# Hybrid streaming-encoder block on one core: the two halves of the normed input, element by element beside each other

## What is computed

```python
h = x + 0.5 * rmsnorm(swiglu(rmsnorm(x, g1), w_gate, w_up, w_down), g1_post)     # D_FF = 5632
z = rmsnorm(h, g_mix) @ w_in                                                     # 2048 x 5120
y = concat(gelu(gate) * rg_lru(conv4(lru_x)), sc_b * conv3(sc_c * sc_x)) @ w_out
h = h + rmsnorm(y, g_mix_post)
h = h + 0.5 * rmsnorm(swiglu(rmsnorm(h, g2), w_gate2, w_up2, w_down2), g2_post)
```

## Time and profile before

| | |
|---|---|
| median of 2 runs | 1818.22 us (1818.16 to 1818.27) |
| the profiled execution, its span | 1816.7 us |
| PE busy | 1799.5 us, 99% of the span, 8066 matmuls |
| PEld busy | 1486.2 us, 82%, 8066 weight loads |
| DVE busy | 940.9 us, 52% |
| ACT busy | 847.9 us, 47% |
| POOL busy | 20.2 us, 1% |
| HBM | 341.91 MB read, 189 GB/s over the span; DMA engines 61% |

### The profile page before, as it was taken

One profiled execution on the slowest core, in us unless ns is written; L12 is line 12 of the kernel. 1 busy time (PEld: TensorE's weight loads), 2 busy tenths in 40 slices (PEclk: granted clock), 3 DMA queues, 4 the chain that ended last, 5 costly groups with the idle time before them and its releaser, 6 DMA issues.

```text
span 1816.7 us, 22683 instructions
## 1 busy us (share of the span) xinstructions
PE 1799.5 (99%) x8066; PEld 1486.2 (82%) x8066; DVE 940.9 (52%) x990; ACT 847.9 (47%) x1023; POOL 20.2 (1%) x21
## 2 busy tenths in 40 slices
PE   8999999999999999999999999999999999999998
PEld 6888888888888888788888878888888888888886
DVE  5545444454454445655686465545445445445444
ACT  6544444444434334566654456444444444434442
POOL 0000000000000000100000010000000000000000
PEclk9999999999999999999999999999999999999999
DMA  7666666666565566675565656666666666556554
GB/s 229 215 191 193 190 188 193 186 188 192 176 199 189 171 203 204 188 211 173 164 196 174 199 160 231 186 189 192 185 186 191 189 187 192 176 177 216 189 184 148
DMA packets 179189, 344.69 MB, mean 190 GB/s; under 512 B 10685, under 2 KB 12869, under 8 KB 178757
## 3 DMA queue, kind: packets, MB, share of 16 engines
q1 hardware_dynamic: 179108, 344.04, 60.7%
q10 hardware_dynamic: 32, 0.01, 0.0%
HBM read 341.91 MB, written 2.10 MB: 189 GB/s over the span
## 4 chain that ended last, share of the span: by engine, by line
PE 98%; ACT 0%; DVE 0%; DMA 0%; issue 0%; POOL 0%; DVEq 0%; SPq 0%; ACTq 0%
PE ps L858 32%; PE ps L860 32%; PE ps L859 32%; PE ps L945 1%; PE ps L894 1%; PE ps L986 0%; PE ps L998 0%; DMA resid<-in_x 0%; DVE xT_lo L617 0%; ACT xT_hi L405 0%; POOL rstd L340 0%; ACT w_hi L383 0%; ACT act_g L387 0%; DVE resid L607 0%; DVEq L96 0%
## 5 line engine op out<-in xcount | busy, mean ns | idle before, releaser
L583 DVE TENSOR_TENSOR w_lo<-raw,w_hi 128x1024 fp32r<-128x1024 f32 x636 | 776.5, 1224 | 824.2 <-ACT w_hi L383 821.2
L383 ACT CAST w_hi<-raw 128x1024 fp32r<-128x1024 f32 x640 | 670.3, 1053 | 853.6 <-PE ps L860 829.5
L858 PE MATMUL ps<-w_hi,xT_hi 128*128 128x512 f32 x1728 | 679.0, 393 | 2.5 <-DVE xT_lo L617 2.5
L860 PE MATMUL ps<-w_hi,xT_lo 128*128 128x512 f32 x1728 | 674.0, 390 | 0.0
L859 PE MATMUL ps<-w_lo,xT_hi 128*128 128x512 f32 x1728 | 673.4, 390 | 0.0
L858 PEld LDWEIGHTS ps<-w_hi,xT_hi 128*128 128x128 f32 x1728 | 325.0, 188 | 69.1 <-issue 3.3
L860 PEld LDWEIGHTS ps<-w_hi,xT_lo 128*128 128x128 f32 x1728 | 324.9, 188 | 68.5
L859 PEld LDWEIGHTS ps<-w_lo,xT_hi 128*128 128x128 f32 x1728 | 325.1, 188 | 66.2
L858 PE MATMUL ps<-w_hi,hT_hi 128*128 128x512 f32 x832 | 327.5, 394 | 0.0
L860 PE MATMUL ps<-w_hi,hT_lo 128*128 128x512 f32 x832 | 326.3, 392 | 0.0
L859 PE MATMUL ps<-w_lo,hT_hi 128*128 128x512 f32 x832 | 323.6, 389 | 0.0
(11 more groups left out here) (77 smaller groups left out, 314.7 us busy)
## 6 DMA issues: line engine op xcount, KB each, us to landing
raw<-in_ffn_w_gate SPq DMA_DIRECT2D x176, 512.0 KB, 4.4
raw<-in_ffn_w_up SPq DMA_DIRECT2D x176, 512.0 KB, 3.5
raw<-in_ffn_w_down SPq DMA_DIRECT2D x176, 512.0 KB, 4.8
raw<-in_w_in SPq DMA_DIRECT2D x80, 512.0 KB, 3.8
raw<-in_w_out SPq DMA_DIRECT2D x32, 512.0 KB, 4.8
resid<-in_x SPq DMA_DIRECT2D x8, 256.0 KB, 8.8
gpost<-in_ffn_post_g SPq DMA_DIRECT2D x2, 1024.0 KB, 6.5
out<-resid SPq DMA_DIRECT2D x8, 256.0 KB, 2.8
```

The costliest lines, as they stand in the source:

```text
L383: sc.copy(w_hi[:, s], raw[:, s]).then_inc(hi_ready, 1)
L583: ve.tensor_tensor(w_lo[:, s], raw[:, s], w_hi[:, s].bitcast(f32), ALU.subtract).then_inc(lo_ready, 1)
L858: te.matmul(dst, xh, w_hi[:, s, k], start=start and k == 0, stop=False)
L860: last = te.matmul(dst, xl, w_hi[:, s, k], start=False, stop=stop and k == GK - 1)
```

## The change

The two tensors become two views of one. Element 0 of the last, innermost dimension is the high half and element 1 the low half of the same number:

```diff
@@ -104,8 +104,8 @@
         raw = sb("raw", [P, SLOTS, GK, W])
         w_hi = sb("w_hi", [P, SLOTS, GK, W], f32r)
         w_lo = sb("w_lo", [P, SLOTS, GK, W], f32r)
-        xT_hi = sb("xT_hi", [P, KD, T], f32r)
-        xT_lo = sb("xT_lo", [P, KD, T], f32r)
+        xT = sb("xT", [P, KD, T, 2], f32r)
+        xT_hi, xT_lo = xT[:, :, :, 0], xT[:, :, :, 1]
         resid = sb("resid", [P, TOK, D])
         gpost = sb("gpost", [P, D])
         act_g = sb("act_g", [P, TOK, W])
```

## The result

The changed kernel takes 1850.24 us (median of 2 runs, 1849.93 to 1850.56) where the kernel before took 1818.22. The ratio is 1.0179, with a 95% interval of 1.0161 to 1.0196: 32.0 us more, slower beyond doubt, though by a little under 2%. The profiled execution has a span of 1848.1 us, 31.4 us more than before's.

The account below looks back on a forecast made before the run. The prediction took the kernel as bound by PE's stream of matmuls. It summed 1816.7 + 0 for the loads + 1 for the writes = 1817.7 us profiled, so 1819 for timed runs, range 1815 to 1892.

Parts of the forecast that it names:

- What bounds the kernel: Whole kernel: one stream of matmuls on PE, busy 99%; each nanosecond of distance is paid 5184 times with xT.
- (a): Weight loads of 5184 xT matmuls get a stride of 8 bytes: still hidden behind a matmul, cost taken as zero.
- one column per two cycles: Estimated reading rate of an ordinary 4-byte weight load: 101 to 107 ns of its 188 ns record, the rest latency.
- Rival B: Weight loads from xT no longer hide behind a matmul: at full size 524 us more, 2343 us; chance 0.12.
- the walking rate: Strided load walks 9.6 bytes per ns of each partition, as the moving operand and the transpose's load already do.
- the forecast: Whole kernel: 1819 us, own range 1815 to 1832, loads and matmul distance unchanged; chance 0.57 with D in it.
- Rival A: xT weight loads take turns from the moving stream; stride doubles the loss, 55 to 70 us more, 1873 to 1889; chance 0.27.
- fixed price of switching stationary operands: Matmul distance: the 13.5 ns not streaming were said not to be this, since head products take 216 ns each.
- it depends on addresses or timing a little: Said of the loss per matmul, from distances of 229.2 ns with hT and 226.8 with xT.
- (b): Strided writes of L405 and L617 in the hand-overs: 1 us taken, bounds zero and 14.2 us.
- Rival D: Hand-overs grow by the full 14.2 us of the strided writes: 1832 us; chance included in the forecast's 0.57.
- Rival C: Matmul stream gains because the stride breaks an address pattern: at best 55 us, 1763 us; chance 0.04.

Follow-up runs that it names:

- experiment 6: Probe without a block: series of 24 matmuls, many with 128 moving columns so loads aren't covered; stride 1 took 110 ns, 2 118, 3 174, 4 235.
- experiment 5: Changed kernel with halves of two feature tiles beside each other, so xT loads have a stride of 16 bytes: 1866.08 us, ratio 1.0267 to the kernel before.
- the first probe: No block, only series of 24 matmuls varying load columns, strides and types: fp32r with 512 moving columns 227 ns contiguous, 233 ns at stride 2.
- experiment 4: Operand starts shifted in a probe and two kernels: 64 unused bytes before hT in the kernel before, 1812.26 us; xT 128 bytes later in the changed kernel, 1840.87 us.
- the third probe: The probe of experiment 6: matmul series without a block; with 128 moving columns, 110 ns at stride 1 and 118 at stride 2.
- the second probe: No block, matmul series with shifted operand starts and other moving-column counts: contiguous loads 227 to 233 ns, stride 2 233.3 ns at nine of ten starts.

## Why the prediction was right in its range and wrong in its centre

**What bounds the kernel**: right. PE's busy time took up the whole of the 31.4 us, and each nanosecond was paid nearly 5184 times; outside the first chunks, 4896 times.

**(a) The load still hides**: right. It needs 110 ns contiguous and 118 at a stride of 8 bytes (experiment 6), so "one column per two cycles" held roughly. No run tests the other half of that estimate, 53 ns for a transpose's load. The argument that even a doubled load (2 x 107 = 214 ns) would fit under 227 was too kind: the doubled load of experiment 5 needs 233. Rival B was empty at this change's stride.

**(a) The price of zero**: this is the step that failed. I took zero because "the walking rate is one that the rows show twice, and nothing shows that the loss belongs to the load". The rate was met, nearly: the record grew by 6 ns only. But a rate that each of two streams reaches says nothing of how they get on together at full speed, and there the cost was 6.5 ns per matmul. The sum should have had 4896 x 6.5 = 32 us in this place.

**The range held by its width.** 1850 lies above the forecast's own range (1815 to 1832) and below A's (1873 to 1889): no mechanism of the prediction gives it. It is inside 1815 to 1892 only because that range joins the two, and "within 2%" held by 0.2 of a point.

**Rival A**: its direction was right, its mechanism and size were not. I had read the loss of 13.5 ns as proportional to what the load touches and said it is no "fixed price of switching stationary operands". The probes show 13.3 ns for every fp32r matmul with 128 stationary columns and 256, 320, 384 or 512 moving ones at the best place, and no less with short loads: a fixed amount at these counts, for fp32r alone, since bfloat16 and float32 lose only 2.5 ns (215.8 against 213.3). At 512 columns the stride adds 6.6 ns to that, about half of what A gave; it adds 3 at 480, takes 2.5 away at 448, and does nothing at 256, 320 and 384. The reading that "it depends on addresses or timing a little", which I drew from 229.2 against 226.8 ns, was the better clue. It was the place of hT, and moving hT by 64 bytes removed it.

**The skill's rules**: the port rule of "TensorE: Matmul & The Clock Gate" ("Step-by-step: what each phase is for"), that a load takes nothing from the running matmul, disagrees with the runs for fp32r: stride and start of the load alone moved the distance between 227 and 233 ns. The measurement decides. For bfloat16, where only strides were tried and no other starts, the probes agree with that rule and with the page's 216 ns. The line rule of "SBUF — State Buffer" ("Door 1: The DMA port swizzle"), two hits in 16 bytes suffice, fits the load's own time (110, 118, then 233 ns) and the writes (DVE 344, 344, then 452 ns), but doesn't tell that the running matmul is disturbed. For the moving operand the runs disagree with it: at a stride of 8 bytes, two hits in 16 bytes, its matmul took 452 ns for 227 (L107 of the first probe).

**(b) The writes**: right. DVE's kept 344 ns, ACT's grew by 9 ns, PE's wait for xT went from 2.5 to 2.6 us. Rival D and its 14.2 us were empty.

**Rival C**, a gain by another place, was empty for the stride. That places matter was true, though: experiment 4 found its gain in hT.

**What would show it**: the tests named for A were a round of 46.5 to 47 us with loads of 188 ns, for the forecast 44.4. The round came out at 45.67, between the two.

Open: what the 13.3 ns are, and what exactly collides. The runs show the stride's cost only with a moving operand of four bytes per cycle at the upper clock level; at the lower level strided matmuls start 427 ns apart, the bare columns (L79 of the third probe). It depends on the starts and on the number of moving columns, and spreads to neighbouring matmuls. They don't show the place in the memory or in PE where it happens.

## What to carry to other kernels

Where matmuls run back to back at full rate, a load that is hidden in the profile can still slow the matmul that hides it: for fp32r with 512 moving columns, keep the stationary operands contiguous and start them at a multiple of 256 bytes from the moving ones. A stride on the moving operand is far dearer (452 ns for 227). Read the distance of starts, compare it with the pure streaming time, and where two products of the same shape differ by even 1%, as 229 and 227 ns did here, look at their addresses first. A cost that each instruction pays may not be additive over instructions, so measure the real sequence and not one instruction.

## What the runs showed of the hardware

Granted clock in the windows of the third probe (us, busy by engine, granted clock):

```profile
48.00:52.00 4.00, 4.00 (x26) 4.00 (x26) 0.00 (x0) 0.00 (x0) 1.00 0.00 0
52.00:58.30 6.30, 6.30 (x30) 6.30 (x30) 0.00 (x0) 0.00 (x0) 0.60 0.00 0
58.30:64.00 5.70, 5.70 (x16) 4.52 (x16) 0.00 (x0) 0.00 (x0) 0.54 0.00 0
```

From 43.08 on, four series with 128 moving columns ran, all with loads that outlast their matmuls. In the fourth, at stride 4, the granted clock fell to the lower level, 1.2 GHz, while PE counts as busy throughout. A mean of 0.60 over 52.00 to 58.30 puts the fall at 53.3, soon after that series began at 52.71, so it can't be put down to the stride of 4 alone. The next series, of 512 columns, then started about the first half of its 24 matmuls 427 ns apart. So loads that outlast their matmuls can cost twice, though in the second probe, with 256 moving columns and loads that need 233 ns, the clock stayed at 1.00. An fp32r matmul of 256 columns takes 120 ns and one of 512 takes 227, so splitting one in two costs 13 ns more. And 64 bytes of unused memory were worth 5.3 us against the kernel before on the same chip (1817.59 us).
